# Recurrence rates one round ahead, key work from GpSimd to VectorE, filler products, and forward transforms from even and odd times

## The reference

```python
# layer 0, RWKV-7: 16 heads of 64; two directions z
a = sigmoid(a0[z] + (xa @ a1[z]) @ a2[z])            # rates
kk = k * k_k;  kk = kk / norm(kk)                    # unit keys, per head
k_dir = k * (1.0 + (a - 1.0) * k_a)                  # keys of each direction
# scan over tokens, S is 64x64 per head and direction:
#   sa = S @ (-kk);  S = S * decay + sa (x) (kk * a) + v (x) k_dir;  y = S @ r
bonus = sum(r * (k_dir[0] + k_dir[1]) * r_k) * v
out = ((layernorm(y) * ln_w + ln_b + bonus) * g) @ wo
# layer 1, Hyena: two convolutions by FFT of length 512
y = irfft(rfft(u, n=512) * rfft(kern))[:256] + u * skip
z = x1 * conv(v, kern0);  y = x2 * conv(z, kern1)
# after each mixer: 4 groups x 8 experts, top group, top 2 experts of it
logits = rms_norm(x) @ router_w + router_b
out = sum over 2 experts of weight * ((silu(h @ w_gate) * (h @ w_up)) @ w_down)
```

## Time and profile before

| | us |
|---|---|
| median of 3 runs | 2000.03 (1995.26 to 2000.1) |
| the profiled execution | 2007.12 |
| its span in the trace | 2005.2 |

### The profile page before, as it was taken

One profiled execution on the slowest core, in us unless ns is written; L12 is line 12 of the kernel. 1 busy time (PEld: TensorE's weight loads), 2 busy tenths in 40 slices (PEclk: granted clock), 3 DMA queues, 4 the chain that ended last, 5 costly groups with the idle time before them and its releaser, 6 DMA issues. The chain is left out here.

```text
span 2005.2 us, 34229 instructions
## 1 busy us (share of the span) xinstructions
PE 1776.6 (89%) x13939; PEld 949.0 (47%) x13939; DVE 769.8 (38%) x1862; ACT 541.1 (27%) x1001; POOL 110.6 (6%) x93
## 2 busy tenths in 40 slices
PE   5778797887978796999999999798997999999996
PEld 2345555545545544443444443476554444443442
DVE  5666575676676534510110010374645300110101
ACT  3234443543544312111111111313311111111111
POOL 0012102102012000000000000000000000000000
PEclk8979998999988997999999999899998999999999
DMA  9013322323333438999999998331454999999993
GB/s 301 25 34 98 93 75 86 104 86 95 91 94 102 148 102 344 396 426 428 428 428 428 429 428 351 112 109 57 175 239 202 427 428 429 429 428 428 428 420 124
DMA packets 105168, 504.04 MB, mean 251 GB/s; under 512 B 15568, under 2 KB 60352, under 8 KB 79184
## 3 DMA queue, kind: packets, MB, share of 16 engines
q1 hardware_dynamic: 103728, 501.88, 62.9%
q10 hardware_dynamic: 1312, 0.37, 0.1%
HBM read 501.13 MB, written 1.09 MB: 250 GB/s over the span
## 5 line engine op out<-in xcount | busy, mean ns | idle before, releaser
L2001 DVE TENSOR_TENSOR arena<-banks,arena 128x512 f32<-128x512 f32 x32 | 22.1, 692 | 659.2 <-PE banks L1816 659.2
L1816 PE MATMUL banks<-arena 128*64 128x512 f32 x1024 | 226.3, 594 | 9.6 <-DMA arena<-in_moe_w_up 9.5
L1838 PE MATMUL banks<-arena 128*64 128x512 f32 x1024 | 226.8, 595 | 3.3 <-ACT arena L1932 3.3
L1807 PE MATMUL banks<-arena 128*64 128x512 f32 x1024 | 225.3, 592 | 3.3 <-DVE arena L1924 3.3
L796 PE MATMUL banks<-arena 128*128 128x512 f32 (+1 forms) x384 | 158.5, 550 | 0.8 <-ACT arena L1105 0.8
L1816 PEld LDWEIGHTS banks<-arena 128*64 128x64 f32 x1024 | 81.7, 137 | 152.2 <-issue 152.2
L1807 PEld LDWEIGHTS banks<-arena 128*64 128x64 f32 x1024 | 74.3, 137 | 147.8 <-issue 144.2
L1838 PEld LDWEIGHTS banks<-arena 128*64 128x64 f32 x1024 | 70.7, 137 | 154.5 <-issue 150.7
L1926 ACT ACTIVATE arena<-banks,arena 128x128 f32<-128x128 f32 x128 | 48.2, 457 | 338.9 <-PE banks L1796 338.9
L1796 PEld LDWEIGHTS banks<-arena 128*128 128x128 f32 x1024 | 121.1, 198 | 28.1 <-issue 24.3
L1796 PE MATMUL banks<-arena 128*128 128x128 f32 x1024 | 127.2, 284 | 3.5 <-DVE arena L1996 3.5
(11 more groups left out here) (393 smaller groups left out, 2465.6 us busy)
## 6 DMA issues: line engine op xcount, KB each, us to landing
arena<-in_moe_w_gate SPq DMA_DIRECT2D x64, 2048.0 KB, 14.9
arena<-in_moe_w_up SPq DMA_DIRECT2D x64, 2048.0 KB, 17.1
arena<-in_moe_w_down SPq DMA_DIRECT2D x64, 2048.0 KB, 13.1
arena<-in_ada_w SPq DMA_DIRECT2D x128, 192.0 KB, 2.9
arena<-in_ada_w SPq DMA_DIRECT2D x64, 256.0 KB, 3.6
arena<-in_rw_wrkv SPq DMA_DIRECT2D x24, 512.0 KB, 5.1
arena<-in_hy_w_in SPq DMA_DIRECT2D x6, 2048.0 KB, 8.7
arena<-in_ada_w SPq DMA_DIRECT2D x8, 1024.0 KB, 17.2
```

The lines of the kernel that those rows point to most:

```text
L1807: mm = pe.matmul(G[j * CAP:(j + 1) * CAP, :], xT[:, t, j * CAP:(j + 1) * CAP], wg[par][j][:, t], start=(t == 0), stop=(t == KT - 1))
L1816: mm = pe.matmul(U[j * CAP:(j + 1) * CAP, :], xT[:, t, j * CAP:(j + 1) * CAP], wu[j][:, t], start=(t == 0), stop=(t == KT - 1))
L1838: mm = pe.matmul(bank[j * CAP:(j + 1) * CAP, :], hT[:, t, j * CAP:(j + 1) * CAP], wd[j][:, t, half * 512:(half + 1) * 512], start=(t == 0) ...
L2001: dve.tensor_tensor(h, U[:, :], sg, ALU.mult).then_inc(h_ready, 1)
```

## The change

- *Rates ahead.* `low_rank` a0, a1 and `rate_rank` go from slot 0 of the block's round to slot 14 of the round before (there called block q), behind `from_values_early` and `spread`; their place in `open_order` goes with them, between `wyc` and `t1`. `BB` becomes two buffers.
- *Keys on VectorE.* GpSimd's `keys` is gone with its three semaphores; VectorE does the same in `key_rates` (slot 0), `key_products` (slot 1, behind `rates`), `key_sum` (slot 4) and `bonus` (slot 6). The features move one slot later (3, 4, and both `features_kr` in 5), `row_scales` from 5 to 6. TensorE's and ScalarE's `rows` of block m - 1 go from slot 6 to 7. SyncE's `load_first` waits for `rg` of block n instead of a1.
- *Fillers.* `keep_warm(pe, bank, count)` multiplies the identity with constants into a bank that is free, `count` times; nobody reads it. Two at the end of the heads and two at the end of the convolutions, four in each router behind the logits, four behind the last scatter of layer 0, four ahead of the Hyena layer's first transposes of normalized rows.
- *Router.* VectorE copies the turned rows before it waits for the squares of the norm, not after.
- *Convolutions.* The transform of a half makes only the first 128 frequencies of the even times and of the odd times, each in a bank of its own: four products instead of eight. ScalarE copies the two even banks; VectorE adds and subtracts even and odd parts into `vhat`, which gives the two tiles of frequencies. The copies use the space of `half_b`, so ScalarE waits for the end of the previous half's products (`imag_ready`), and `half_a` serves twice, with one drain more.

```diff
@@ -87,6 +87,11 @@
         return self.sems[-1]
+    def keep_warm(self, pe, bank, count):
+        for _ in range(count):
+            pe.matmul(bank[:, :], self.c("ident"), self.const[:, 0:512], start=True, stop=True)
@@ -516,7 +521,6 @@
         order += [(m, u) for u in ("bl", "kl") if chain]
-        order += [(m + 1, u) for u in ("a0", "a1") if now]
@@ -528,6 +532,7 @@
         order += [(m + 1, u) for u in ("wyc",) if now]
+        order += [(m + 2, u) for u in ("a0", "a1") if early]
@@ -591,7 +596,7 @@
     AR = [[s.take(3 * L) for _ in range(2)] for _ in range(2)]
-    BB, KK = s.take(STEPS, 2, C), s.take(STEPS, 2, C)
+    BB, KK = [s.take(STEPS, 2, C) for _ in range(2)], s.take(STEPS, 2, C)
...
@@ -697,7 +702,7 @@
                     if slot == 2 and 0 <= n and n + 1 < CH:
-                        sp.wait_ge(open_done, OPEN.done(n, "a1"))
+                        sp.wait_ge(open_done, OPEN.done(n, "rg"))
@@ -735,33 +740,7 @@
-            def keys(n):
-                pool.wait_ge(ka_ready, 1)
-                pool.wait_ge(open_act, OPEN.taken(n, "a1")[1])
...
-                pool.sem_inc(bon_ready, 1)
             for n in range(CH):
-                keys(n)
...
@@ -1002,11 +981,8 @@
                     if chain and slot == 0:
-                        turn(m, "bl", BB, 1)
+                        turn(m, "bl", BB[m % 2], 1)
                         turn(m, "kl", KK, 1)
-                    if now and slot == 0:
-                        low_rank(n, "a0")
-                        low_rank(n, "a1")
@@ -1021,10 +997,11 @@
                         products_early(n)
-                    if behind and slot == 6:
+                    if chain and slot == 7:
+                        level_two_z(m, 1)
+                    if behind and slot == 7:
                     if chain and slot == 7:
-                        level_two_z(m, 1)
...
@@ -1047,6 +1024,9 @@
                         from_values_early(n)
+                    if early and slot == 14:
+                        low_rank(q, "a0")
+                        low_rank(q, "a1")
@@ -1083,6 +1063,7 @@
                 project_out(CH - 1, k)
+            s.keep_warm(pe, s.psum[0], 2)
@@ -1106,7 +1087,7 @@
                 bank = read(n, f"a{z}")
-                act.activation(steps(BB, z), chunks(bank[:, :]), ACT.Sigmoid, bias=vec(2 + z, n)).then_inc(open_act, 1)
+                act.activation(steps(BB[n % 2], z), chunks(bank[:, :]), ACT.Sigmoid, bias=vec(2 + z, n)).then_inc(open_act, 1)
...
@@ -1263,6 +1241,9 @@
                         spread(n)
+                    if early and slot == 14:
+                        rate_rank(q, 0)
+                        rate_rank(q, 1)
@@ -1323,11 +1304,33 @@
+            def key_rates(n):
+                dve.wait_ge(open_act, OPEN.taken(n, "a1")[1])
+                if n:
+                    dve.wait_ge(open_done, OPEN.done(n - 1, "kl"))
+                dve.tensor_scalar(KK, BB[n % 2], vec(5, n), ka1[:, n:n + 1], ALU.mult, ALU.add)
+                dve.drain()
             def rates(n):
-                dve.wait_ge(av_read, n + 1)
                 for z in range(2):
-                    dve.tensor_tensor(steps(BB, z), steps(BB, z), chunks(kk), ALU.mult)
-                dve.drain()
+                    dve.tensor_tensor(steps(BB[n % 2], z), steps(BB[n % 2], z), chunks(kk), ALU.mult)
+            def key_products(n):
+                dve.wait_ge(open_act, OPEN.taken(n, "k")[1])
+                for z in range(2):
+                    dve.tensor_tensor(steps(KK, z), steps(KK, z), chunks(kT), ALU.mult)
+                dve.drain()
+            def key_sum(n):
+                if n >= 3:
+                    dve.wait_ge(open_done, OPEN.done(n - 3, "rows"))
+                to = bon[n % 3].rearrange("p (j t) -> p j t", t=C)
+                dve.tensor_tensor(to, last_steps(KK, 0), last_steps(KK, 1), ALU.add)
+            def bonus(n):
+                dve.tensor_tensor(bon[n % 3], bon[n % 3], rT, ALU.mult)
+                dve.drain()
+                dve.tensor_scalar(bon[n % 3], bon[n % 3], vec(8, n), None, ALU.mult).then_inc(bon_ready, 1)
@@ -1335,19 +1338,17 @@
                 dve.scalar_tensor_tensor(late(n % 2, z, 0), half(kk, 1), -1.0, half(ea, 1), ALU.mult, ALU.mult)
-                dve.tensor_tensor(steps(BB, z), steps(BB, z), chunks(eb), ALU.mult)
+                dve.tensor_tensor(steps(BB[n % 2], z), steps(BB[n % 2], z), chunks(eb), ALU.mult)
                 if z == 0:
-                    dve.wait_ge(bsum_ready, n + 1)
                     dve.drain()
-                    dve.wait_ge(bon_ready, n + 1)
@@ -1547,26 +1548,31 @@
                         chain_close(m, j)
+                    if now and slot == 0:
+                        key_rates(n)
                         rates(n)
-                    if now and slot == 2:
-                        features(n, 0)
+                        key_products(n)
                     if now and slot == 3:
+                        features(n, 0)
+                    if now and slot == 4:
                         features(n, 1)
+                        key_sum(n)
+                        dve.drain()
                         row_variances(m - 1)
-                    if now and slot == 4:
-                        dve.drain()
+                    if now and slot == 5:
                         features_kr(n, 0)
-                    if now and slot == 5:
                         features_kr(n, 1)
-                    if behind and slot == 5:
+                    if behind and slot == 6:
                         row_scales(m - 1)
+                    if now and slot == 6:
+                        bonus(n)
@@ -1867,6 +1873,7 @@
             logits(1, turned_act, xT1)
+            s.keep_warm(pe, X0, 4)
@@ -1898,6 +1905,8 @@
             scatter(pe, PAIRS - 1, 1, stop=True)
+            if hyena is not None:
+                s.keep_warm(pe, G, 4)
@@ -2015,11 +2024,11 @@
             dve.tensor_tensor(router_s, router, sc.unsqueeze(2).to_broadcast([P, KT, NL]), ALU.mult).then_inc(router_ready, 1)
-            dve.wait_ge(squares_done, 1)
-            dve.tensor_scalar(small[:, :, 1:2], small[:, :, 0:1], 1.0 / D, NORM_EPS, ALU.mult, ALU.add).then_inc(var_done, 1)
             dve.tensor_copy(xT[:, 4:8].rearrange("p a b -> p (a b)"), X1[:, :]).then_inc(turned_dve, 1)
+            dve.wait_ge(squares_done, 1)
+            dve.tensor_scalar(small[:, :, 1:2], small[:, :, 0:1], 1.0 / D, NORM_EPS, ALU.mult, ALU.add).then_inc(var_done, 1)
@@ -2424,6 +2433,7 @@
             pe.transpose(s.psum[7][:, 128:144], rows2[0:16, :], s.c("ident")[0:16, 0:16]).then_inc(chv_done, 1)
+            s.keep_warm(pe, s.psum[0], 4)
@@ -2603,7 +2613,8 @@
         ("vT_done", "vt_ready", "dft_done", "vhat_ready", "real_ready", "imag_ready", "y_done", "y_ready"))
-    o_done, skip_ready = S("o_done"), S("skip_ready")
+    o_done, skip_ready, half_ready = S("o_done"), S("skip_ready"), S("half_ready")
+    half_even = [half_b[:, part] for part in range(2)]
@@ -2631,14 +2642,12 @@
                     pe.wait_ge(vt_ready, od * 4 + 2 * half + 2)
-                    for n in range(4):
-                        part, ft = n // 2, n % 2
+                    for part in range(2):
                         if od or half:
-                            pe.wait_ge(vhat_ready, (od * 2 + half) * 4 + n - 3)
+                            pe.wait_ge(vhat_ready, (od * 2 + half - 1) * 2 + part + 1)
                         for i in range(TT):
-                            mm = pe.matmul(s.psum[4 + n][:, :], fwd[part][:, i, ft * P:(ft + 1) * P],
-                                           vt[:, i, half * 512:(half + 1) * 512], start=(i == 0), stop=(i == TT - 1))
-                        mm.then_inc(dft_done, 1)
+                            pe.matmul(s.psum[4 + part * 2 + i][:, :], fwd[part][:, i, 0:P],
+                                      vt[:, i, half * 512:(half + 1) * 512], start=True, stop=True).then_inc(dft_done, 1)
...
@@ -2678,10 +2688,11 @@
                         act.activation(vt[:, i, c], s.psum[half * 2 + i][:, :], ACT.Copy).then_inc(vt_ready, 1)
-                    for n in range(4):
-                        part, ft = n // 2, n % 2
-                        act.wait_ge(dft_done, (od * 2 + half) * 4 + n + 1)
-                        act.activation(vhat[:, part, ft, c], s.psum[4 + n][:, :], ACT.Copy).then_inc(vhat_ready, 1)
+                    for part in range(2):
+                        act.wait_ge(dft_done, (od * 2 + half) * 4 + part * 2 + 1)
+                        if od or half:
+                            act.wait_ge(imag_ready, od * 2 + half)
+                        act.activation(half_even[part], s.psum[4 + part * 2][:, :], ACT.Copy).then_inc(half_ready, 1)
@@ -2691,15 +2702,23 @@
                     c = slice(half * 512, (half + 1) * 512)
-                    dve.wait_ge(vhat_ready, (od * 2 + half) * 4 + 4)
+                    for part in range(2):
```

(12 more changed lines are left out.)

39 lines of the change are left out of this document (8 added, 31 removed).

## The result

The changed kernel takes 1972.66 us (median of 4 runs, 1971.11 to 1975.86), the kernel before 1999.49 (median of 4). The ratio is 0.9872 with a 95% interval of 0.9854 to 0.9891: 26.8 us less by the medians, 25.6 (21.8 to 29.2) by the ratio. The forecast was 34 us less, 1966, in a range of 1950 to 1990. The direction and the range hold. The gain is some 8 us smaller than forecast, 7 by the medians.

A forecast was written before the change was run, and what follows sets the result against it. It took TensorE's waits in the heads, 9.0 of a 29.2 us window per round, as the main place to gain; heads 21, convolutions 5, routers and fillers 8 make 34 us off 2000.0: 1966, range 1950 to 1990.

The forecast's parts named there:

- heads: Recurrent heads, 581 us with TensorE busy 83%: 21 us less over all rounds, bounds 5 and 33.
- convolutions: Both convolution orders: halved transform takes 14 us off TensorE, 5 arrive as VectorE becomes the bound; bounds 2 and 8.
- routers and fillers: Both routers: fillers raise the clock and the reordered wait saves 0.9 us each; 8 us less, bounds 1 and 11.
- The window of slots 0 to 6: Heads, round's first step to first products_late: 29.2 us becomes 24.0, a gain of 5.2 per round.
- The wait on GpSimd turns into one on VectorE: Same window: TensorE idles 2.7 us before step 2 and 1.9 before products_early, instead of 2.46 and 0.87.
- Slot 14: Heads: moved rate products and their banks delay the key projection, 2.3 us lost per round, from 1.6 to 3.5.
- Round 0: Heads' first round, no block behind: window 21.75 us becomes 20.2, gain 1.5 less 2.3 for slot 14, -0.8.
- The sum over the rounds: Heads: round 0 -0.8, rounds 1 to 5 gain 14.5, round 6 gains 5.2, start costs 2; 21 us.
- the gather: Routers: the first gather takes 3.9 us, its duration inside the loop, instead of 6.38.
- Slot 14 takes it back: Rival: key projection waits 4 us or more, heads gain only 7, total 20: 1980; chance 0.23 together with another rival.
- Slower: Rival: VectorE bounds every round, its new passes costing GpSimd-like times, rounds lose 2 to 3 us: 2010; chance 0.06.
- More: Rival: clock stays full through each round's first third, 7 us per round, heads 34, total 47: 1953; chance 0.12.

The follow-up runs named there:

- experiments 2: Kernel before with only the heads' edits (rates ahead, keys on VectorE), no fillers: 18.0 us less than the kernel before (14.0 to 22.2).
- experiment 9: Changed kernel without any of its keep_warm fillers, the router's reordered wait kept: 28.2 us less than the kernel before (24.2 to 32.4).
- 5: Kernel before with only the rates moved ahead, key work left on GpSimd: 9.4 us less than the kernel before (5.6 to 13.0).
- 7: Changed kernel with row_variances moved behind the features, slot 5 instead of 4: 31.4 us less than the kernel before (27.6 to 35.4).
- 8: Changed kernel with unread products in TensorE's waits in slot 6 and between the convolutions' halves: 40.0 us less than the kernel before (35.8 to 44.2).
- Experiment 10: Changed kernel with variances later and fillers in slot 6, the convolutions and slots 14 and 15: 1950.8 us, 53.4 less than the kernel before.
- experiment 4: Kernel before with only the fillers and the router's reordered wait: 6.0 us less than the kernel before (3.4 to 8.8).
- 6: Kernel before with only the key work moved to VectorE, rates left in slot 0: 17.6 us less than the kernel before (12.2 to 23.0).
- experiments 3: Kernel before with only the convolutions' edit: 3.2 us less than the kernel before (0.2 to 6.0).

## Why the prediction was right, and where it was too high

Parts forecast and measured, in us: heads 21 and 18.0 (14.0 to 22.2); convolutions 5 and 3.2 (0.2 to 6.0); routers and fillers 8 and 6.0 (3.4 to 8.8). All three lie within their bounds and all three below the value taken.

- **The window of slots 0 to 6: right to 0.3 us, the clock by luck.** 24.0 forecast, 23.71 measured; the features forecast at 17.4 us from the round's start, TensorE takes them up at 17.2 (395.92 less 378.72). The waits were forecast as 2.7 and 1.9 us for VectorE and are 3.06 and 1.74; 1.0 on ScalarE and it is 1.45. "The wait on GpSimd turns into one on VectorE" is what the timeline shows. Two terms were off and cancel. Between 394.6 and 401.4 and between 408.2 and 411.7 TensorE was busy for 3.8 and 3.4 us at a grant of 0.50 before; afterwards it is so for 5.1 us (394.2 to 401.0). At half clock half of that is lost, so I estimate 3.6 us before and 2.6 after, where the sum had 1.7 and 0.9.
- **Slot 14: right, with a cost missed behind it.** 2.3 us forecast; step 4 to 5 is 2.2 longer. That the two waits there (1.24 and 0.76 us) also lower the clock for the key projection (3.04 us where it was 1.98) was not in the sum; it costs 0 to 2 us in step 5 to 6, 0.2 to 0.5 on average in the profiles of experiments 2 and 9 and of the change, 0.9 to 1.2 in those of 5, 7 and 8. Experiment 10, with three fillers there, doesn't have it.
- **Round 0: the step that failed.** 1.5 us were forecast for its window; it takes 21.76 us as before. Its clock is 0.84 where it was 0.92: it had no wait for row means to lose. Step 0 to 1 gains 2.6 us there too, but behind it TensorE now waits 1.85 and 1.74 us for VectorE, the slow stretch follows, and step 2 to 3 takes 11.97 us instead of 9.56. Over the whole round 0.8 us of loss were forecast and the means show 4.3.
- **The sum over the rounds: terms too low and too high.** By the same means rounds 1 to 5 gain 3.7 us each (2.9 forecast) and round 6 6.0 (5.2); the start gains 1.5 (2 forecast). With round 0 that is 22 us up to the last step, near the forecast of 21, but 4 us too much in the rounds stand against 3.5 too little in round 0. The timed 18.0 (14.0 to 22.2) is lower and has the 22 at its upper end.
- **Convolutions: the replay was right, the clock was left out of the sum (it stood in the lower bound alone).** VectorE starts adding at 5.3 us (5.4 forecast), the real part of the second half is done at 23.1 (23.1), TensorE's gap is 3.25 us (3.4). But the transform back behind this gap takes 8.64 and 8.86 us instead of 7.46: the clock is 0.50 from 1391.3 to 1394 and back at 1.00 by 1396. The order ends at 31.6 and 30.2 us where 30.5 and 28.6 were forecast. The mechanism was named ("the stage becomes VectorE's"), the term that was mis-sized is the price of a gap: not the idle time alone.
- **Routers: the gather was right in one of two.** 3.84 us in layer 0 as forecast (3.9), 5.22 in layer 1, where the rank products still ran at a mostly full clock but the grant was 0.50 again when the gather began:

```profile
1478.30:1480.10 1.80, 0.08 (x1) 0.00 (x0) 1.37 (x5) 0.00 (x0) 0.00 (x0) 0.87 0.00 0
1480.10:1482.00 1.90, 1.86 (x8) 1.86 (x9) 0.00 (x0) 0.00 (x0) 0.00 (x0) 0.50 0.03 9
```

The wait of 1.76 us between them, for VectorE's selection, stands in both layers; in layer 0 the clock stayed at 1.00 through it. So a filler ahead of one wait isn't sure to hold through the next, and over all profiles it held in three of twelve gathers (experiment 9). The reordering gave its 0.9 and 1.0 us. In the stretches the fillers give 6.9 us, where 6 were taken; in the time 4.1 (1.5 to 6.9) by experiment 4, and less than that only by the ratio of experiment 9, which is not explained.
- **The rivals.** *Slot 14 takes it back* was right in its place and wrong in its size for the whole (18, not 7); it describes what the move of the rates does inside a round with both neighbours: its gain of 2.6 us in step 0 to 1 is paid for in steps 4 to 6. *Slower* fell: VectorE's passes cost 0.61 to 0.81 us, not GpSimd's 1.2 to 1.7. *More* fell for this change, since the clock drops again; experiment 10 is what it described, the clock full through the first third of rounds 1 to 6.
- **What I had put down to the wrong edit.** The forecast credits the window's gain to the rates and the keys together. Experiments 2, 5 and 6 take them apart: the keys on VectorE give 17.6 us alone, the rates ahead 9.4 alone, both 18.0 (14.0 to 22.2). The larger part is the keys'; whether the two add in part is within the intervals.

## What to carry to other kernels

When an engine's wait disappears, sum up the queue of the next engine that the same work waits for, and price each remaining gap of TensorE at its own length plus what the work behind it costs at the clock granted then: here 2 us on top of a pair of gaps of 3.06 and 1.74 us. Where such a gap can't be closed, products that nobody reads can fill it, if they end before the wait does; they gave 9 to 14 us here, a third to over a half as much as the whole change. And before moving work ahead to an emptier place, measure the move both alone and on top of the rest: here it gave 9.4 us alone and nothing certain on top of the keys, since inside a round it was paid for where it went and only round 6, which has no next rates to make, came out ahead.

## What the runs showed of the hardware

- Elementwise work on GpSimd beside VectorE cost more than VectorE doing both: 3.5 us for four passes of 128x512 on the two engines, 2.5 us for the same four on VectorE.
- A VectorE pass of 128x1024 float32 with two scalars per partition takes 0.81 us, with one 0.75.
- The granted clock fell to 0.50 behind a wait of 3.25 us in the convolutions in six of eight cases (not in the second order of experiments 3 and 7, 7.45 and 7.46 us), and behind two waits of 3.06 and 1.74 us with only eight small products between them; with products in the gaps that nothing reads it stayed at 1.00. It came back up during the work behind each gap.
- Two executions of one kernel can differ by 9 us in their profiles at the same place of the program, while single steps (3 to 4: 9.34) agree to 0.01 us: a stage's difference between two profiles is to be believed only where it repeats in each round.
